# Router logits on four column groups, with start products and three smaller edits, in a two-model kernel on one Trainium2 core

## The chip, the cores and the metric

The kernel runs on one core of one Trainium2 chip. The metric is the device time of one execution in microseconds; lower is better. Everything is float32. TensorE handles a float32 product in several passes, which the trace keeps as two matmul records and two weight loads per product; a transpose has one of each.

## The reference, cut to what matters

Two models run one after the other on a sequence of 256 tokens of width 1024.

```python
def reference(...):
    x = first_block(x, ...)      # two hybrid layers: gated delta rule beside attention, LN, conv FFN, LN
    return second_block(x, ...)  # one layer: differential + dilated attention, then 16 experts

# inside second_block
x = x + jnp.concatenate([oa, od], axis=-1) @ w_out[l]
x = x + expert_choice_ffn(rms_norm(x, norm2_g[l]), w_router[l], w_gate[l], w_up[l], w_down[l])
return rms_norm(x, norm_f_g)

def expert_choice_ffn(h, w_router, w_gate, w_up, w_down):
    aff = jax.nn.softmax((h @ w_router).astype(jnp.float32), axis=-1)   # [1, 256, 16]
    g, idx = lax.top_k(aff.transpose(0, 2, 1), cap)                     # cap = 32 tokens per expert
    ...  # each expert: silu(xe @ wg) * (xe @ wu) @ wd, scaled by g, added at idx
```

The hidden width of an expert is 2816, so the weights of one expert are 34.6 MB and those of all 16 make up most of what the kernel reads.

## The kernel before, in words

Each engine has its own hand-written list of instructions; semaphores alone order them. Tokens are held as two tiles of 128 rows (`t` = 0, 1), channels as eight tiles of 128 (`k`). `x` holds rows, `xT` the transposed rows. PSUM is used as eight banks of 512 float32 columns, `ps[0]` to `ps[7]`.

**Start.** SyncE (queue SP) issues the first weights in an order written out: the first block of `first_in` (`first_columns`), half of `x_t` (`xT_in1`), the second block (`second_columns`), two more blocks (`slot_in0`), then the streams of `w_in` (line 375), unit 2 first, then unit 1 and unit 3. Only then come the convolution's coefficients `conv_w` (line 412, `conv_in`) and small vectors. TensorE starts in `first_products` (lines 823 to 838): it waits for the first columns, forms 16 products of 256 columns (line 826), 16 more (line 813), one for a table of biases (line 831), and 16 for unit 2 (line 676); then come the gate logits (line 901, 32-column weights), the first piece of dense work (line 861) and the key products (line 916). ScalarE waits for `conv_in` before its first tap (line 1482). VectorE first copies the bias table (line 1871), waits for `conv_in` too, and then runs the other taps (line 1881), on which the SiLU and the key products at line 916 depend.

**Around the router.** After the attention of the second model, TensorE forms the output product of tile 0 (into banks 2, 3), then that of tile 1 (banks 6, 7), line 1261, with the transposes of tile 0 (line 1236) inside. VectorE adds both halves of a tile to `x` (line 2208), ScalarE squares and copies the first transposed half (line 1648), VectorE the second (line 2211), and then applies the norm to 1024 columns (`rms`, line 2149) for the gather. `logits` (line 1244) holds 128 transposed tokens stationary and streams the 16 columns of `router_w`, eight products a tile. Then VectorE's `router_bias` (line 2219), ScalarE's Exp (line 1690), VectorE's `affinities` (line 2228), TensorE's two transposes (line 1270), VectorE's copies (line 2237) and the search of the 32 best of 256 (lines 2242 to 2248). TensorE fills waits with products whose result nobody reads (`keep_clock`, line 1251): one of 512 columns before the transposes, four behind them. The choice is transposed (line 1277), rows are gathered (line 1290), and expert 0 begins at line 1348.

**Experts.** 16 times: gate and up products (line 1348), 32 token columns stationary on each of four column groups, then the down products (line 1316), in two halves. Weights come in pieces of 5.6 MB into four slots; a DMA is issued when its slot's last reader (`piece_used`, for expert 0 also `first_columns_used`) is done. In the last expert the second half of the down weights comes in four transfers of 4, 4, 2 and 1 row blocks (`LAST_ROWS`, line 508), and TensorE waits for each.

The end: the placed rows (line 1404), the last norm (lines 1643 and 2154), the store.

Of the kernel before, what the change touches and what calls it, by code (L numbers as in the profile page):

```python
# [12 lines left out]
P = 128  # L13
S = 256
# [70 lines left out]

HID_BANKS, OUT_BANK = (3, 4, 6), (4, 0)


def constants():
# [35 lines left out]
    parts["slot"] = np.broadcast_to((np.arange(P) % CAP)[None, :] + 1, (P, P))  # L125
    at, cols = {}, 0
# [42 lines left out]
def build(nc, a, out, scratch, CAT):  # L169
    ctx = ExitStack()  # L170
    with ctx:
# [125 lines left out]
        normed_rows = second_scratch.take(T, D)  # L297
        out_quarters = second_scratch.take(D // 4)
        BIAS_BEFORE = 2 * H * 3 * P - T * D - D // 4
# [51 lines left out]
        def _(sp):  # L351
# [39 lines left out]
            for l in range(DEPTH):  # L391
# [12 lines left out]
                first_blocks(2, 4).then_inc(sem("slot_in0"), 16)  # L404
                for u in (2, 1) + tuple(range(3, len(UNITS_IN))):
                    name = UNITS_IN[u]
                    stream(l, u, columns(a["w_in"], l, OFF[name], AB_COLUMNS if name == "ab" else 512, u))
                    if u == RING - 1:

                        if l:  # L410
                            sp.wait_ge(sem("x_rows"), at(l, "x_rows", 2))
                        sp.dma_start(conv_w, a["conv_columns"][l]).then_inc(sem("conv_in"), 16)
# [231 lines left out]
        def _(pe):  # L644
# [586 lines left out]
            def rows_transposed(t):  # L1231

                pe.wait_ge(sem("second_rows"), t + 1)
                for kh in range(2):
# [4 lines left out]
            def logits(t, ks):  # L1239

                if ks[0] == 0:
                    pe.wait_ge(sem("h2_copied"), 2 * t + 2)
# [11 lines left out]
            for t in range(T):  # L1254
                for k in range(4):
                    if t == 0:
                        pe.wait_ge(sem("attended_read"), at(L, "attended_read", k + 1))
                    elif k == 1:
                        rows_transposed(0)
                    for nh in range(2):  # L1260
                        last = mm(ps[ROWS_BANKS[2 * t + nh]][:, :], mixT[:, 4 + k, t * P:(t + 1) * P], slot(7, 1024)[:, k, nh * 512:(nh + 1) * 512], start=(k == 0), stop=(k == 3))
                last.then_inc(sem("rows_used" if t else "rows_t0"), 2 if t else 1)
# [45 lines left out]
            def keep_clock_on_rows():  # L1308

                mm(ps[1][:, :], ident, normed_rows[:, 0, 0:512], start=True, stop=True)  # L1310
# [16 lines left out]
            def expert(n_, ahead):  # L1327
# [102 lines left out]
        def _(act):  # L1430
# [203 lines left out]
            def rms(n, t):  # L1634
# [3 lines left out]
                elif n == 1:  # L1638
                    act.wait_ge(sem("second_rows"), t + 1)
# [6 lines left out]
                if n == 1:  # L1646
                    act.wait_ge(sem("h2_transposed"), 2 * t + 1)
# [68 lines left out]
        def _(v):  # L1716
# [148 lines left out]

            for l in range(DEPTH):
# [332 lines left out]
            v.drain()  # L2199
            def second_rows(t):  # L2200
# [3 lines left out]
                else:  # L2204
                    v.wait_ge(sem("rows_used"), (DEPTH + 1) * ROW_UNITS + 2)
                for nh in range(2):
                    xs = x[:, t, nh * 512:(nh + 1) * 512]
                    last = w.tensor_add(xs, xs, ps[ROWS_BANKS[2 * t + nh]][:, :])
                last.then_inc(sem("second_rows"), 1)
                v.wait_ge(sem("h2_transposed"), 2 * t + 2)  # L2210
                w.tensor_copy(xT[:, 4:8, t * P:(t + 1) * P], ps[H2_BANKS[2 * t + 1]][:, :].rearrange("p (x y) -> p x y", y=P)).then_inc(sem("h2_copied"), 1)
                if t == 1:
                    router_bias(0)
                rms(1, t, normed_rows, "h2_rows")

            def router_bias(t):

                v.wait_ge(sem("logits"), t + 1)
# [130 lines left out]
```

## Time and profile before

| what | value |
|---|---|
| time, median of 3 runs | 2191.35 us (2190.85 to 2191.48) |
| time of the profiled execution | 2190.44 us |
| its span, first to last instruction | 2188.7 us |
| TensorE busy, share of the span | 1678.1 us, 77% |
| VectorE busy | 644.2 us, 29% |
| ScalarE busy | 310.7 us, 14% |
| read from memory | 692.77 MB |
| mean granted TensorE clock | 0.876 |

The span runs from the first to the last instruction; the execution's own time has 1.7 us around it. A share of busy time is a mean over stages with different limits: TensorE sets the pace up to about 945 us, the weights' transfers after it. In rows of the timeline the columns are start, duration, engine, line, operation, result and operand shape, count, and in brackets the idle time before with what ended it. In rows of windows "PEclk" is the clock granted to TensorE, 1.00 for 2.4 GHz and 0.50 for 1.2 GHz.

### The profile page before, as it was taken

To read this page: it belongs to the slowest core of one execution; us is meant where nothing else is said; L and a number is where in the kernel's file an instruction comes from. 1 tells how busy PE (TensorE), PEld (TensorE's weight loads), DVE (VectorE), ACT (ScalarE), POOL (GpSimd) and SP (SyncE) were. 2 spreads that over 40 slices of the span, in tenths; PEclk is the share of its full clock that TensorE was granted. 3 is DMA by queue.
4 is the path that set the end of the run, shared out by engine and by line. 5 is a ranking of instruction groups with operands and counts; after the bars stand their busy time and mean duration, and the time that the engine had idled before them with its cause. 6 is when DMAs were issued, how large, how long until landed. Compare 5 with 4: busy or idle time off the path is not lost.

```text
span 2188.7 us, 30640 instructions
## 1 busy us (share of the span) xinstructions
PE 1678.1 (77%) x13062; PEld 968.0 (44%) x13062; DVE 644.2 (29%) x1520; ACT 310.7 (14%) x739; POOL 255.5 (12%) x221
## 2 busy tenths in 40 slices
PE   8999999999999999995665565665656466466566
PEld 7867994886799476441221221221122122122122
DVE  3345777545477734320110010010010010010011
ACT  3231220324122013310000000000000000000001
POOL 0003880001388000000000000000000000000000
PEclk9999999999999999987777777777787777778778
DMA  8234652723554275489999999999999999999998
GB/s 316 79 116 145 215 181 96 255 79 116 164 173 175 96 263 235 200 374 430 433 433 434 431 427 434 435 435 434 433 426 433 435 435 434 434 431 427 435 434 345
DMA packets 99943, 695.12 MB, mean 318 GB/s; under 512 B 7627, under 2 KB 53067, under 8 KB 85773
## 3 DMA queue, kind: packets, MB, share of 16 engines
q1 hardware_dynamic: 96304, 684.71, 76.0%
q0 software_dynamic: 1712, 5.35, 0.7%
q10 hardware_dynamic: 1836, 3.80, 0.5%
q8 instruction: 64, 1.05, 0.2%
q14 instruction: 27, 0.21, 0.0%
HBM read 692.77 MB, written 4.22 MB: 318 GB/s over the span
## 4 chain that ended last, share of the span: by engine, by line
DMA 49%; PE 48%; DVE 1%; SPq 1%; ACT 1%; issue 0%; DVEq 0%; ACTq 0%
DMA arena<-in_gate_up 32%; DMA arena<-in_down_rows 17%; PE bank L1123 11%; PE bank L702 6%; PE bank L861 6%; PE bank L1348 6%; PE bank L676 3%; PE bank L1316 2%; PE bank L856 1%; PE bank L1182 1%; PE bank L1063 1%; PE bank L1186 1%; PE bank L1083 1%; PE bank L766 1%; PE bank L813 1%; PE bank L1209 1%
## 5 line engine op out<-in xcount | busy, mean ns | idle before, releaser
L1348 PE MATMUL bank<-arena 128*32 128x512 f32 (+1 forms) x3072 | 441.9, 741 | 366.0 <-DMA arena<-in_gate_up 365.5
L1348 PEld LDWEIGHTS bank<-arena 128*32 128x32 f32 x3072 | 112.5, 139 | 690.5 <-DMA arena<-in_gate_up 395.6
L2290 DVE TENSOR_TENSOR arena<-arena,bank 64x256 f32<-64x256 f32 x96 | 51.3, 535 | 766.3 <-ACT arena L1696 764.7
L1316 PE MATMUL bank<-arena 128*32 128x256 f32 x2816 | 204.5, 458 | 68.6 <-DMA arena<-in_down_rows 68.6
L1123 PE MATMUL bank<-arena 128*128 128x128 f32 x2128 | 238.0, 274 | 0.0
L1123 PEld LDWEIGHTS bank<-arena 128*128 128x128 f32 x2128 | 237.8, 192 | 0.0
L1316 PEld LDWEIGHTS bank<-arena 128*32 128x32 f32 x2816 | 101.0, 130 | 175.4 <-DMA arena<-in_down_rows 86.3
L861 PE MATMUL bank<-arena 128*128 128x256 f32 x576 | 138.6, 387 | 0.0
L1696 ACT ACTIVATE arena<-bank 64x512 f32<-64x512 f32 (+1 forms) x48 | 23.2, 550 | 809.0 <-PE bank L1348 809.0
L702 PE MATMUL bank<-arena 128*128 128x512 f32 x308 | 133.2, 592 | 0.0
L861 PEld LDWEIGHTS bank<-arena 128*128 128x128 f32 x576 | 104.7, 189 | 18.9 <-issue 4.6
L702 PEld LDWEIGHTS bank<-arena 128*128 128x128 f32 x308 | 57.8, 189 | 73.2 <-issue 70.1
L676 PE MATMUL bank<-arena 128*128 128x128 f32 (+1 forms) x704 | 87.0, 285 | 1.4 <-DVE arena L1770 1.4
L676 PEld LDWEIGHTS bank<-arena 128*128 128x128 f32 x704 | 84.1, 191 | 5.1 <-DVE arena L1770 2.6
L2126 DVE SCALAR_TENSOR_TENSOR arena<-bank,arena 128x254 f32<-128x254 f32 (+1 forms) x176 | 76.8, 478 | 24.8 <-ACT arena L1615 18.7
L1615 ACT ACTIVATE arena<-bank,arena 128x256 f32<-128x256 f32 x88 | 45.0, 562 | 139.0 <-DVE bank L2109 119.2
L536 POOL TENSOR_TENSOR arena<-arena 128x512 f32<-128x512 f32 x38 | 49.6, 1305 | 101.4 <-PE bank L1083 71.9
L1358 PE MATMUL bank<-arena 128*128 128x128 f32 x96 | 24.4, 342 | 48.3 <-DVE arena L2290 48.3
L539 POOL TENSOR_TENSOR arena<-arena 128x512 f32<-128x512 f32 x38 | 53.7, 1413 | 0.0
L2295 DVE COPY arena<-bank 64x256 f32<-64x256 f32 x16 | 6.9, 430 | 155.5 <-PE bank L1316 155.5
L538 POOL TENSOR_TENSOR arena<-arena 128x512 f32<-128x512 f32 x38 | 49.2, 1295 | 13.9 <-issue 8.6
L541 POOL TENSOR_TENSOR arena<-arena 128x512 f32<-128x512 f32 x38 | 49.6, 1306 | 5.4
(322 smaller groups left out, 1595.0 us busy)
## 6 DMA issues: line engine op xcount, KB each, us to landing
arena<-in_gate_up SPq DMA_DIRECT2D x60, 5632.0 KB, 46.2
arena<-in_down_rows SPq DMA_DIRECT2D x29, 5632.0 KB, 46.1
arena<-in_w_up SPq DMA_DIRECT2D x44, 1024.0 KB, 7.8
arena<-in_w_in SPq DMA_DIRECT2D x36, 1024.0 KB, 9.3
arena<-in_w_down SPq DMA_DIRECT2D x16, 1024.0 KB, 6.9
arena<-in_gate_up SPq DMA_DIRECT2D x5, 2816.0 KB, 12.3
arena<-in_w_out SPq DMA_DIRECT2D x12, 1024.0 KB, 6.1
arena<-in_w_down SPq DMA_DIRECT2D x12, 512.0 KB, 3.7
```

What stands on the lines that cost most here:

```text
L536: nc.gpsimd.tensor_tensor(s1, w[:, 0:4, cg], w[:, 4:8, cg], ALU.add)
L538: nc.gpsimd.tensor_tensor(s2, s1, w[:, 0:4, cv], ALU.subtract)
L539: nc.gpsimd.tensor_tensor(w[:, 0:4, cg], w[:, 0:4, cv], w[:, 0:4, cg], ALU.subtract)
L541: nc.gpsimd.tensor_tensor(s4, w[:, 4:8, cv], s2, ALU.subtract)
L676: last = mm(ps[bank][:, j * S + lo:j * S + lo + n], w[:, k, c:c + P], xT[:, k, lo:lo + n], start=(k == 0), stop=(k == KT - 1))
L702: return mm(ps[PRODUCT_BANK[m]][:, :], left, right, start=(i == 0), stop=(i == KP - 1))
L861: last = mm(ps[bank][:, j * S:(j + 1) * S], slot(u, 512)[:, k, c:c + P], xT[:, k, :], start=(k == 0), stop=(k == KT - 1))
L1123: last = mm(ps[pair[b]][:, at_ * P:(at_ + 1) * P], left[:, k, :], right[:, k, :], start=(k == 0), stop=(k == 3))
L1316: done = mm(ps[5][32 * q:32 * q + 32, 0:256], hidden_t[:, r, 32 * half:32 * half + 32], weights[:, r - shift, 256 * q:256 * q + 256], star ...
L1348: last = mm(ps[b][32 * q:32 * q + 32, 0:n], expert_x[:, k, :], weights[:, c:c + n], start=(k == 0), stop=(k == KT - 1))
L2126: last = w.scalar_tensor_tensor(ff_conv[:, j % 3, gv, s:S], from_, conv_w[:, 48 + c:49 + c], ff_conv[:, j % 3, gv, s:S], ALU.mult, ALU.add)
L2290: last = w.tensor_mul(hidden[64 * odd:64 * odd + 64, 2 * b:2 * b + m, :], blocks(expert_gate[0:64, c0:c0 + n]), blocks(ps[b][64:P, 0:n]))
```

## The change

Five edits are made together.

1. The logits. `router_w` (16 columns) becomes stationary on four column groups of the array, and 128 columns of `xT` stream past it. Channel tile `k` goes to group `k % 4`, so that four partial sums lie in partitions 0, 32, 64 and 96 of bank `2 + t`, columns 256 to 383. VectorE copies them out (`partials_copied`); one product with the copy stationary and a table of zeros and ones `by_group` adds the four and turns them. VectorE zeroes that part of the two banks once. The output product of tile 1 is ordered by halves of 512 columns, and each half is added and transposed by itself; VectorE takes ScalarE's copy for tile 1.
2. `keep_clock(1)` ahead of the affinities' transposes becomes `keep_clock(1, 2)`, 256 columns for 512.
3. Six products of zeros at the start (five of 256 columns, one of 128), after VectorE has set 256 columns of `zeros`.
4. For the first layer `conv_w` is loaded ahead of the `w_in` streams.
5. In the last expert three products of 512 columns, read by nobody, stand between the first and the second of the four groups of down products.

```diff
+START_PRODUCTS = (S, S, S, S, S, P)
+    parts["by_group"] = (i % 32 == np.arange(NE)[None, :]) * 1.0
...
                 first_blocks(2, 4).then_inc(sem("slot_in0"), 16)
+                if l == 0:
+                    sp.dma_start(conv_w, a["conv_columns"][l]).then_inc(sem("conv_in"), 16)
...
+                pe.wait_ge(sem("zeros_ready"), 1)
+                for n in START_PRODUCTS:
+                    mm(ps[7][:, 0:n], zeros[:, 0:P], zeros[:, 0:n], start=True, stop=True)
                 pe.wait_ge(sem("first_columns"), 16)
...
+            def rows_transposed(t, half=None):
+                for kh in range(2) if half is None else (half,):
+                    pe.wait_ge(sem("second_rows"), t + 1 + (kh if t else 0))
...
+            def partial_logits(t, ks):
+                pe.wait_ge(sem("h2_copied"), 2 if t == 0 else 4 if ks[0] == 0 else 5)
                 for k in ks:
-                    last = mm(ps[2 + t][:, 0:NE], xT[:, k, t * P:(t + 1) * P], router_w[:, k, :], start=(k == 0), stop=(k == KT - 1))
+                    g = 32 * (k % 4)
+                    last = mm(ps[2 + t][g:g + NE, S:S + P], router_w[:, k, :], xT[:, k, t * P:(t + 1) * P], start=(k < 4), stop=(k >= 4))
...
+            def logits(t):
+                pe.wait_ge(sem("h2_copied"), 3 * t + 3)
+                mm(ps[2 + t][:, 0:NE], logit_parts[:, t * P:(t + 1) * P], table("by_group"), start=True, stop=True).then_inc(sem("logits"), 1)
...
+            for nh in range(2):
                 for k in range(4):
+                    if nh == 0 and k == 2:
                         rows_transposed(0)
+                    if nh == 1 and k == 1:
+                        partial_logits(0, range(KT))
+                    last = second_product(1, k, nh)
+                if nh == 0:
+                    last.then_inc(sem("rows_t0"), 1)
+            last.then_inc(sem("rows_used"), 2)
+            rows_transposed(1, 0)
+            logits(0)
+            rows_transposed(1, 1)
+            partial_logits(1, range(4))
+            partial_logits(1, range(4, KT))
+            logits(1)
+            keep_clock(1, 2)
-            logits(0, range(6))
-            rows_transposed(1)
-            logits(0, range(6, KT))
-            logits(1, range(KT))
-            keep_clock(1)
...
                             last = down_rows(half, rows_, r0, n)
+                            if i == 0:
+                                for _ in range(3):
+                                    keep_clock_on_rows(4)
...
+            w.memset(zeros, 0.0).then_inc(sem("zeros_ready"), 1)
...
+            def partials_copied(t):
+                v.wait_ge(sem("logits"), 2 * t + 1)
+                w.tensor_copy(logit_parts[:, t * P:(t + 1) * P], ps[2 + t][:, S:S + P]).then_inc(sem("h2_copied"), 1)
...
+                    if t and nh == 0:
+                        partials_copied(0)
+                if t == 0:
+                    v.drain()
+                    w.memset(banks[:, 512 * 2:512 * 4].rearrange("p (b n) -> p b n", b=2)[:, :, S:S + P], 0.0)
+                    v.drain()
+                for kh in range(2):
+                    if t or kh:
+                        v.wait_ge(sem("h2_transposed"), 2 * t + kh + 1)
+                        w.tensor_copy(xT[:, 4 * kh:4 * kh + 4, t * P:(t + 1) * P], ps[H2_BANKS[2 * t + kh]][:, :].rearrange("p (x y) -> p x y", y=P)).then_inc(sem("h2_copied"), 1)
                 if t == 1:
+                    partials_copied(1)
                     router_bias(0)
                 rms(1, t, normed_rows, "h2_rows")
```

## Rows read from the trace of the kernel before

**Rows 1.** The chain that ended last, in order of time: start, duration, what.

```profile
15.64 11.49 DMA arena<-in_conv_columns
...
964.81 39.26 DMA arena<-in_gate_up
```

**Rows 2.** The timeline of the start, all engines, parts of the first 46 us.

```profile
1.27 0.42 SPq L400 DMA_DIRECT2D arena<-in_x_t  x1
...
5.79 9.74 PE L826 MATMUL bank<-arena 128*128 128x256 f32 x32 [5.79 <-DMA arena<-in_first_in]
...
15.37 7.09 PE L813 MATMUL bank<-arena 128*128 128x256 f32 x32
...
23.46 0.68 DVE L1871 COPY arena<-bank 12x512 f32<-12x512 f32 x1 [23.46 <-PE bank L831]
...
27.16 1.57 ACT L1482 ACTIVATE arena<-bank,arena 128x256 f32<-128x256 f32 x4 [10.26 <-DMA arena<-in_conv_columns]
...
28.11 8.10 DVE L1881 SCALAR_TENSOR_TENSOR arena<-bank,arena 128x255 f32<-128x255 f32 x18 [3.98 <-ACT arena L1482]
...
30.48 1.08 PE L901 MATMUL bank<-arena 128*32 128x256 f32 x16
...
34.26 1.15 PE L916 MATMUL bank<-arena 128*64 128x64 f32 x32 [0.22 <-ACT arena L1494]
```

**Rows 3.** Windows inside line 826: busy times with records, granted clock, DMA share, GB/s.

```profile
6.00:11.00 5.00, 5.00 (x12) 3.96 (x13) 0.00 (x0) 0.00 (x0) 0.00 (x0) 1.00 1.01 379
11.70:15.00 3.30, 3.30 (x17) 2.89 (x16) 0.00 (x0) 0.00 (x0) 0.00 (x0) 1.00 1.05 397
```

**Rows 4.** The DMA issue of the second half of x_t: size, us to landing.

```profile
arena<-in_x_t SPq DMA_DIRECT2D x1, 512.0 KB, 7.1
```

**Rows 5.** The timeline around the router, 928 to 942 us.

```profile
928.01 1.29 DVE L2208 TENSOR_TENSOR arena<-arena,bank 128x512 f32<-128x512 f32 x2 [1.51 <-PE bank L1261]
...
930.48 0.69 DVE L2211 COPY arena<-bank 128x512 f32<-128x512 f32 x1 [1.19 <-PE bank L1236]
...
931.65 1.29 DVE L2149 SCALAR_TENSOR_TENSOR arena<-arena 128x1024 f32<-128x1024 f32 x1
...
933.64 0.17 DVE L2219 TENSOR_REDUCE arena<-bank 128x1 f32<-128x16 f32 x1 [0.71 <-PE bank L1244]
...
934.82 0.23 DVE L2228 TENSOR_SCALAR arena<-arena 128x16 f32<-128x16 f32 x1
...
935.29 0.63 PE L1270 MATMUL bank<-arena 128*16 128x128 f32 x2
...
935.72 5.44 PE L1251 MATMUL bank<-arena 128*128 128x512 f32 x8
...
935.75 0.49 DVE L2237 COPY arena<-bank 16x128 f32<-16x128 f32 x2 [0.70 <-PE bank L1270]
...
941.09 0.29 PE L1277 MATMUL bank<-arena 16*128 16x16 f32 x2
```

**Rows 6.** Two windows of the same stretch; columns as in rows 3.

```profile
929.00:932.50 3.50, 2.94 (x26) 2.74 (x26) 2.15 (x6) 3.07 (x5) 0.00 (x0) 1.00 1.05 410
932.50:935.90 3.40, 3.40 (x12) 2.04 (x12) 1.62 (x8) 1.05 (x5) 0.00 (x0) 0.51 1.01 417
```

**Rows 7.** The timeline of the last expert's second half of down products.

```profile
2132.79 1.75 SPq L508 DMA_DIRECT2D arena<-in_down_rows  x4
...
2170.20 1.93 PE L1316 MATMUL bank<-arena 128*32 128x256 f32 x32 [0.44 <-DMA arena<-in_down_rows]
...
2175.10 4.86 PE L1316 MATMUL bank<-arena 128*32 128x256 f32 x56 [2.96 <-DMA arena<-in_down_rows]
```

**Rows 8.** The DMA issues behind it: size, us to landing.

```profile
arena<-in_down_rows SPq DMA_DIRECT2D x1, 1024.0 KB, 43.9
...
arena<-in_down_rows SPq DMA_DIRECT2D x1, 512.0 KB, 44.6
```

**Rows 9.** A window inside the last 56 records; columns as in rows 3.

```profile
2175.50:2178.00 2.50, 2.50 (x28) 1.18 (x24) 0.00 (x0) 0.00 (x0) 0.00 (x0) 0.50 0.36 147
```

More of the change, by code:

```diff
@@ L297, in build @@
         normed_rows = second_scratch.take(T, D)
+        zeros = normed_rows[:, 0, 0:S]
         out_quarters = second_scratch.take(D // 4)
+        logit_parts = out_quarters
         BIAS_BEFORE = 2 * H * 3 * P - T * D - D // 4
@@ L411, in _ @@
                             sp.wait_ge(sem("x_rows"), at(l, "x_rows", 2))
-                        sp.dma_start(conv_w, a["conv_columns"][l]).then_inc(sem("conv_in"), 16)
+                            sp.dma_start(conv_w, a["conv_columns"][l]).then_inc(sem("conv_in"), 16)
                         for i in range(2):
@@ L1253, in _, with second_product @@
             unit_in(L, 7)
-            for t in range(T):
+            def second_product(t, k, nh):
+                return mm(ps[ROWS_BANKS[2 * t + nh]][:, :], mixT[:, 4 + k, t * P:(t + 1) * P], slot(7, 1024)[:, k, nh * 512:(nh + 1) * 512], start=(k == 0), stop=(k == 3))
+            for k in range(4):
+                pe.wait_ge(sem("attended_read"), at(L, "attended_read", k + 1))
+                for nh in range(2):
+                    last = second_product(0, k, nh)
+            last.then_inc(sem("rows_t0"), 1)
+            for nh in range(2):
                 for k in range(4):
-                    if t == 0:
-                        pe.wait_ge(sem("attended_read"), at(L, "attended_read", k + 1))
-                    elif k == 1:
+                    if nh == 0 and k == 2:
                         rows_transposed(0)
-                    for nh in range(2):
-                        last = mm(ps[ROWS_BANKS[2 * t + nh]][:, :], mixT[:, 4 + k, t * P:(t + 1) * P], slot(7, 1024)[:, k, nh * 512:(nh + 1) * 512], start=(k == 0), stop=(k == 3))
-                last.then_inc(sem("rows_used" if t else "rows_t0"), 2 if t else 1)
-            logits(0, range(6))
-            rows_transposed(1)
-            logits(0, range(6, KT))
-            logits(1, range(KT))
-            keep_clock(1)
+                    if nh == 1 and k == 1:
+                        partial_logits(0, range(KT))
+                    last = second_product(1, k, nh)
+                if nh == 0:
+                    last.then_inc(sem("rows_t0"), 1)
+            last.then_inc(sem("rows_used"), 2)
[6 more added lines that the diff above has]
+            keep_clock(1, 2)
             for t in range(T):
@@ L1306, in _, with keep_clock_on_rows @@
             gathered_transposed(1)
-            def keep_clock_on_rows():
-                mm(ps[1][:, :], ident, normed_rows[:, 0, 0:512], start=True, stop=True)
+            def keep_clock_on_rows(bank=1):
+                mm(ps[bank][:, :], ident, normed_rows[:, 0, 0:512], start=True, stop=True)
             def down_rows(half, weights, r0, n, shift=0):
@@ L1645, in rms @@
                     f(normed_rows[:, t, :], x[:, t, :], ACT.Square, accum_out=sum_sq[:, t:t + 1])
-                if n == 1:
-                    act.wait_ge(sem("h2_transposed"), 2 * t + 1)
+                if n == 1 and t == 0:
+                    act.wait_ge(sem("h2_transposed"), 1)
                     f(xT[:, 0:4, t * P:(t + 1) * P], ps[H2_BANKS[2 * t]][:, :].rearrange("p (x y) -> p x y", y=P), ACT.Copy).then_inc(sem("h2_copied"), 1)
@@ L2203, in second_rows @@
                     v.wait_ge(sem("rows_t0"), at(L, "rows_t0", 1))
-                else:
-                    v.wait_ge(sem("rows_used"), (DEPTH + 1) * ROW_UNITS + 2)
                 for nh in range(2):
+                    if t:
+                        v.wait_ge(*((sem("rows_used"), (DEPTH + 1) * ROW_UNITS + 2) if nh else (sem("rows_t0"), at(L, "rows_t0", 2))))
                     xs = x[:, t, nh * 512:(nh + 1) * 512]
                     last = w.tensor_add(xs, xs, ps[ROWS_BANKS[2 * t + nh]][:, :])
-                last.then_inc(sem("second_rows"), 1)
-                v.wait_ge(sem("h2_transposed"), 2 * t + 2)
-                w.tensor_copy(xT[:, 4:8, t * P:(t + 1) * P], ps[H2_BANKS[2 * t + 1]][:, :].rearrange("p (x y) -> p x y", y=P)).then_inc(sem("h2_copied"), 1)
+                    if t or nh:
+                        last.then_inc(sem("second_rows"), 1)
+                    if t and nh == 0:
[8 more added lines that the diff above has]
+                        w.tensor_copy(xT[:, 4 * kh:4 * kh + 4, t * P:(t + 1) * P], ps[H2_BANKS[2 * t + kh]][:, :].rearrange("p (x y) -> p x y", y=P)).then_inc(sem("h2_copied"), 1)
                 if t == 1:
+                    partials_copied(1)
                     router_bias(0)
@@ L2216, in router_bias @@
             def router_bias(t):
-                v.wait_ge(sem("logits"), t + 1)
+                v.wait_ge(sem("logits"), 2 * t + 2)
                 w.tensor_reduce(rmax[:, t:t + 1], ps[2 + t][:, 0:NE], AX.X, ALU.max, negate=True)
```

8 lines of the change are left out of this document (1 added, 7 removed).

## The prediction

> **What bounds the kernel now.** I read the chain of waits first. In the first 16 us it ends in a transfer: the coefficients of the convolution, issued at 15.64 us, landing 11.49 us later. From about 31 to 945 us it is mostly TensorE's products, and from 964.81 us on it alternates between transfers of expert weights, the first of them 39.26 us, and the products that free their slots [rows 1]. So the kernel has two regimes. Up to 945 us whatever shortens TensorE's list moves all behind it. After that, weights flow without a gap; since each transfer is issued when a product has freed a slot, an earlier start of expert 0 moves the whole flow, and a gain inside the flow is worth nothing except behind the last transfer. The change works in three places: the start, the router (928 to 945 us), and the last 20 us. I read the timeline of each, then the landings of the transfers and the granted clock in windows.
>
> **The start: edits 3 and 4.** TensorE begins at 5.79 us. Its first 32 records take until line 813 begins at 15.37 us, 9.6 us, while the next 32 of the same shape take 7.02 us up to the bias product (15.37 + 7.09 less the overlap of the tail), which is 0.44 us a product [rows 2]. The windows say why: 12 records in 5.00 us, then 17 in 3.30 us [rows 3]. The column of the granted clock reads 1.00 in both, so here the counts must be believed and not the column: the first 5.8 us ran at 1.2 GHz. The Trainium skill's page "TensorE: Matmul & The Clock Gate", Part 1, says that the clock is low by default and that the engine's activity releases it; by that rule the operands' values would not matter, and the counts of rows 3 agree with the first half of it.
>
> The zero products need VectorE's memset; VectorE has nothing ahead of it (its first instruction in the trace waits for line 831 and starts at 23.46 us [rows 2]). I take 1.3 us for it to be done, the time at which SP issues [rows 2]. At the low clock a product of 256 columns takes 0.83 us (5.00 us / 12 records, two a product), so five and a half take 4.6 us and end at 5.9 us, where the first columns land: nothing is lost. If the clock is up by then, four products take 1.76 us and end at 7.7 us; the next four need the second half of `x_t`, issued at 1.27 us and landed 7.1 us later [rows 4], at 8.37 us. Twelve products follow: 8.37 + 12 x 0.44 = 13.65 us instead of 15.37, **a gain of 1.7 us**. Its bounds: 0.1 us lost (the fill runs from 5.79 to 5.9 and the clock stays low), and 2.1 us won (0.40 us a product, as 17 records in 3.30 us give).
>
> This gain alone would stop at line 916, the key products: they wait for ScalarE's SiLU with only 0.22 us of idle time for TensorE before them, and that SiLU hangs on the taps of VectorE, 28.11 to 36.21 us, which hang on the coefficients' landing at 27.1 us [rows 1, 2]. Edit 4 removes that. The transfer goes behind four of SP's issues instead of ten; I take the landing at about 13 us from its neighbours (8.37 us for an issue at 1.27). The first tap can then follow the first products at 13.65, and VectorE starts when the bias copy is done, about 22.5 us (23.46 - 1.7 + 0.7). Its 8.1 us of taps end some 4 us earlier than before, where TensorE comes only 1.7 us earlier: line 916 no longer waits. The issues that `conv_w` is moved past, the six of `w_in`, come one small transfer later, 112 KB, about 0.3 us at 397 GB/s [rows 3]; TensorE waits for none of them before 31 us, all its rows there being back to back. So edit 4 is worth 0.2 us by itself and opens the way for the 1.7 of edit 3; I count 1.7 together. Behind it TensorE's list is the chain.
>
> **The router: edits 1 and 2.** Product by product, against the times before. `partial_logits(0)` is put into tile 1's output product. The nearest row is line 901: eight products with 32 stationary columns and 256 moving ones between full products, 1.08 us [rows 2]. Half the columns take away up to 0.44 us: 0.6 to 1.1, I take 0.8. So the product ends at 928.8 instead of 928.0. The page "TensorEngine Tiling (Array Packing)" of the Trainium skill, Tiling Modes, Key Properties, says that a change of the tiling mode drains TensorE, which speaks against this edit; line 901 holds one such pair in its 1.08 us, tile 1's partial products would add a second of some 0.2 us (1.08 less 2 x 0.44), and by that rule edit 1 would gain nothing.
>
> Behind 928.8 only one addition of 0.65 is left (the other went ahead): 929.45, where two took until 929.30 [rows 5]. VectorE then copies both transposed halves, 0.69 each, one of which was ScalarE's: 930.85 against 931.17. The last four partial products and their hop 0.5 (bound 0.3 to 0.6, from half of line 901), their copy 0.28 as half of line 2237's pair: 931.65. From the end of the copy to the end of the norm's 1024 columns it took 1.77 us (931.17 to 932.94) and that stays, because VectorE's list is the same: 933.4, when the second `router_bias` can start. Before, it waited for TensorE's narrow logits until 933.64. So turning the logits gains **0.2 us**, not the 1.9 us by which TensorE's 16 records shrink: VectorE is at once the bound, with the norm of tile 1 in its queue.
>
> Then edit 2. The affinities are ready at 935.05, but the filler product held the transposes until 935.29 and the copies until 935.75 [rows 5]; half as long and started earlier, it is out of the way, and the copies come 0.45 us earlier beside the 0.2. The search of VectorE ends about 0.6 us earlier, at 940.3 or so. But the fill of four products, 935.72 + 5.44 = 941.16, ended with the search, at line 1277 (941.09). It took 5.44 us because the clock, full until 932.5, was 0.51 in the window behind it [rows 6]; at the full clock it would take 3.5. In the new order it starts 0.4 us earlier and ends, with the clock rising when it did, at 940.9. **Edits 1 and 2 together: 0.2 us.** Bounds: 0.8 won, where the search alone decides (clock full), and 1.1 lost, where all four products run at 1.2 GHz from 935.4 us: 4 x 1.7 us, to 942.2. The zeroing of banks 2 and 3 on VectorE costs nothing: it lies where VectorE waits for transposes of tile 0. Later `rows_used` makes SP issue two pieces 0.8 us later; expert 0 needs the first of them only two channel pairs into its products.
>
> **The end: edit 5.** Before the last seven row blocks TensorE was idle for 2.96 us; their 56 records took 4.86 us, to 2179.96, with the clock at 0.50 [rows 7, 9]. At the pace of the 32 before (1.93 us) they would take 3.4. Three products of 0.88 us fit into 2.96. But the transfers bound the gain: of four issues in 1.75 us the third starts at 2133.67 and lands 43.9 later, at 2177.6, the fourth at 2134.1 plus 44.6, at 2178.7 [rows 7, 8]. The first 32 records end at 2177.03, wait, the next 16 end at 2178.5, wait, the last 8 end at 2179.2. **Gain 0.8 us**, not 1.5. Bounds: 0.8, and 0 in an execution whose clock did not fall there.
>
> **The sum.** The profiled execution took 2190.44 us, 1.7 around its span. 2190.44 - 1.7 - 0.2 - 0.8 = 2187.7. The median of the runs lies 0.9 above that execution, so 2188.6 us.
>
> **Rivals.** (a) The router stage gives its bound: the clock does not fall and the search alone decides. 2188.6 - 0.6 = 2188.0. For it: the new order has fewer narrow products. Against it: the window in which the clock was lost had 2.94 us of 3.50 busy [rows 6], and the new order idles more there. (b) Products of zeros don't raise the clock, or not by 8.4 us: edit 3 gives nothing, edit 4 its 0.2: 2188.6 + 1.7 - 0.2 = 2190.1. No row shows a product of zeros. (c) The idle time ahead of the fill keeps the clock low through all four fill products, 1.1 lost instead of 0.2 won: 2189.9. For it: with the fill cut, TensorE stands still about 2 us there. (d) Slower: VectorE's memset comes late. TensorE waits for it before it may touch the first columns, so the start is z + 4.6 us for a memset at z, and line 813 begins at z + 11.6 (16 full-clock products). Against 15.37 this loses from z = 3.8 us, and the whole kernel from z = 4.8; at z = 9, for one, 2188.6 + 1.7 + 5.2 = 2195.5. Only that other engines issue by 1.3 us [rows 2] speaks against it.
>
> **Chances and range.** Forecast 0.58 (its own range 2187.6 to 2189.5); (a) 0.13; (b) 0.12; (c) 0.11; (d) 0.03; 0.03 for a cause that I don't see. All bounds won give 2190.44 - 2.1 - 0.8 - 0.8 + 0.9 = 2187.6; the runs spread by 0.6, and the 1233 us of weights' flow may differ by 0.04%, 0.5: down to 2186.5. Upward (b) and (c) with the same spread: 2190.8. About what a measurement of this kernel can tell from no change is 0.2%, 4.4 us. Nearly all cases lie within: faster by more 0.09 (all bounds and a cause unseen), same 0.87, slower 0.04.
>
> **What would show it.** Line 813 begins near 13.6, with line 826's records short from 8.4 on; line 1482 follows the first products, not a transfer; expert 0 (line 1348) begins near 943.6; line 2219's second record waits for nothing; line 1277 waits for the fill; in the last expert TensorE waits twice more, for the third and the fourth transfer, at a clock of 1.00. I am wrong if line 813 doesn't move, if line 1251's fill grows beyond 6 us, or if the shift of line 916 is lost before 945 us.

## The result and the profile after

The kernel after takes 2198.66 us (median of 7 runs, 2198.38 to 2199.62), the one before 2191.35 (7 runs, 2189.39 to 2194.5): a ratio of 1.0036, 95% interval 1.0026 to 1.0046. It is slower: 7.3 us between the medians, 0.33%. The forecast of 2188.6, its range up to 2190.8 and all four rivals miss it. The span of the profiled execution went from 2188.7 to 2196.8 us.

The first reading is where along the span the 8.1 us arise. Four marks do it: the start of the long dense part (line 1132; line 1123 before; called line 1132 for every kernel below), of tile 0's output product, of expert 0 (line 1373), and of the first of the last four groups of down products (line 1341; line 1316 before).

| stretch | before | after | change |
|---|---|---|---|
| start to line 1132 | 209.54 | 207.75 | -1.8 |
| line 1132 to the output product | 703.60 | 703.53 | -0.1 |
| output product to expert 0 | 32.36 | 31.47 | -0.9 |
| expert 0 to the first of the last four groups | 1224.7 | 1236.7 | +12.0 |
| from there to the end of the last group | 9.76 | 8.64 | -1.1 |

The three places that the change works on all gained. The loss is in the flow of the experts' weights, where the change does nothing until its last 20 us. The chain of waits shows how it is spread. After:

```profile
207.75 118.81 PE bank L1132 x1064
...
942.75 19.14 PE bank L1373 x192
962.05 39.34 DMA arena<-in_gate_up
...
1378.17 5.00 PE bank L1341 x88
...
1540.72 6.69 PE bank L1341 x88
...
1702.56 5.00 PE bank L1341 x88
...
1864.41 6.69 PE bank L1341 x88
```

Before:

```profile
1378.69 6.69 PE bank L1316 x88
...
1538.61 5.00 PE bank L1316 x88
...
1698.53 5.00 PE bank L1316 x88
...
1858.46 5.00 PE bank L1316 x88
```

One pass of the loop handles two experts. Before, it takes 159.92 or 159.93 us, three times over; after, 162.55, 161.84 and 161.85. So every pass pays about 2 us: it is no single stall. The queues of the DMA engines say what differs in a pass. Rows are queue and kind, packets, MB, share of 16 engines; first the window from 1445 to 1605 us of before, one pass long:

```profile
DMA packets 1730, 69.30 MB, mean 433 GB/s; under 512 B 192, under 2 KB 192, under 8 KB 192
...
q1 hardware_dynamic: 1730, 69.30, 100.3%
```

The same window of after:

```profile
DMA packets 1722, 68.95 MB, mean 431 GB/s; under 512 B 186, under 2 KB 186, under 8 KB 186
...
q1 hardware_dynamic: 1713, 68.80, 99.8%
q8 instruction: 9, 0.15, 0.4%
```

Queue q8 is named for instructions; its packets are of 16 KB (0.15 MB / 9). Before, it moved nothing in this pass, nor in any other from 1285 to 2085 us; after, it moves nine packets in each, in a stretch where the weights already take all 16 engines. Over the whole kernel q8 has 64 packets before and 118 after, on the pages of the two profiles. The row of before:

```profile
q8 instruction: 64, 1.05, 0.2%
```

And of after:

```profile
q8 instruction: 118, 1.93, 0.4%
```

The 54 more are six times nine. The loop runs seven times (the last two experts stand behind it), so after each of its six jumps back the body is fetched anew. 12.0 us over six is 2.0 us a pass, as the chain shows.

TensorE's list of instructions gives the cause that I put to the test. By count of the program, one pass of the expert loop is 1687 instructions of TensorE (a float32 product is four, a transpose two, two waits in a row one). The loop begins at instruction 13861 in before and at 13893 in after, 32 later: 24 for the six products of zeros, 8 for the logits' two added products. Nothing inside the loop is changed.

For the places of the change, the timeline of after; columns as in [rows 2]. The start:

```profile
0.88 0.27 DVE L1894 MEMSET arena<- 128x256 f32 x1 [0.88 <-PEq L2365]
1.21 4.49 PE L827 MATMUL bank<-arena 128*128 128x256 f32 x12 [1.21 <-DVE arena L1894]
...
2.94 0.48 SPq L410 DMA_DIRECT2D arena<-in_conv_columns  x1
...
5.79 2.00 PE L835 MATMUL bank<-arena 128*128 128x256 f32 x8
8.52 5.47 PE L835 MATMUL bank<-arena 128*128 128x256 f32 x24 [0.73 <-DMA arena<-in_x_t]
13.83 7.09 PE L819 MATMUL bank<-arena 128*128 128x256 f32 x32
...
22.52 5.41 DVE L1910 SCALAR_TENSOR_TENSOR arena<-bank,arena 128x255 f32<-128x255 f32 x12
...
32.36 1.13 PE L925 MATMUL bank<-arena 128*64 128x64 f32 x32
```

The memset is done at 1.15 us, the zeros' 12 records end at 5.70, as the first columns land, and the 32 records of line 835 (826 before) need 8.2 us with their wait instead of 9.74 [rows 2]. In the kernel without the products of zeros (run 3 below) the same 32 records take 9.26 us. The products of zeros do raise the clock. Around the router:

```profile
923.46 0.63 PE L1253 MATMUL bank<-arena 128*16 128x128 f32 x16
...
926.89 0.80 SPq L452 DMA_DIRECT2D arena<-in_gate_up  x2
...
931.53 0.17 DVE L2263 TENSOR_REDUCE arena<-bank 128x1 f32<-128x16 f32 x1
...
933.10 5.30 PE L1265 MATMUL bank<-arena 128*128 128x512 f32 x8
933.65 0.41 DVE L2286 MAX8 arena<-arena 16x8 f32<-16x256 f32 x1
...
938.33 0.30 PE L1302 MATMUL bank<-arena 16*128 16x16 f32 x2
```

The end, the answer to [rows 7]:

```profile
2179.46 1.93 PE L1341 MATMUL bank<-arena 128*32 128x256 f32 x32
2181.32 2.84 PE L1335 MATMUL bank<-arena 128*128 128x512 f32 x6
2184.09 1.93 PE L1341 MATMUL bank<-arena 128*32 128x256 f32 x32
2186.19 1.07 PE L1341 MATMUL bank<-arena 128*32 128x256 f32 x16 [0.16 <-DMA arena<-in_down_rows]
2187.46 0.64 PE L1341 MATMUL bank<-arena 128*32 128x256 f32 x8 [0.20 <-DMA arena<-in_down_rows]
```

A window inside it, the answer to [rows 9]: the clock is 1.00 where it was 0.50.

```profile
2184.00:2188.00 4.00, 3.64 (x57) 1.50 (x56) 0.00 (x0) 0.00 (x0) 0.00 (x0) 1.00 0.26 102
```

### The profile page after: what moved, and what is told of

The parts are those of the page before. It is cut to its first block, busy times and chain, and to the rows that moved or that the text cites. A ratio compares the mean times of both kernels' runs of the same rounds, so it can differ in the third digit from the quotient of the medians.

```text
span 2196.8 us, 30690 instructions
## 1 busy us (share of the span) xinstructions
PE 1682.7 (77%) x13084; PEld 968.7 (44%) x13084; DVE 645.6 (29%) x1525; ACT 310.6 (14%) x738; POOL 255.7 (12%) x221
## 4 chain that ended last, share of the span: by engine, by line
DMA 49%; PE 49%; DVE 1%; ACT 1%; issue 0%; DVEq 0%; SPq 0%; ACTq 0%
DMA arena<-in_gate_up 32%; DMA arena<-in_down_rows 17%; PE bank L1132 11%; PE bank L870 6%; PE bank L708 6%; PE bank L1373 6%; PE bank L682 3%; PE bank L1341 2%; PE bank L1191 1%; PE bank L865 1%; PE bank L1072 1%; PE bank L1195 1%; PE bank L1092 1%; PE bank L819 1%; PE bank L772 1%; PE bank L1218 1%
## 5 line engine op out<-in xcount | busy, mean ns | idle before, releaser
L542 POOL TENSOR_TENSOR arena<-arena 128x512 f32<-128x512 f32 x38 | 49.6, 1305 | 101.7 <-PE bank L1092 71.9
L545 POOL TENSOR_TENSOR arena<-arena 128x512 f32<-128x512 f32 x38 | 54.1, 1425 | 0.0
L544 POOL TENSOR_TENSOR arena<-arena 128x512 f32<-128x512 f32 x38 | 48.8, 1284 | 13.7 <-issue 8.4
```

What stands on the lines that cost most here:

```text
L542: nc.gpsimd.tensor_tensor(s1, w[:, 0:4, cg], w[:, 4:8, cg], ALU.add)
L544: nc.gpsimd.tensor_tensor(s2, s1, w[:, 0:4, cv], ALU.subtract)
L545: nc.gpsimd.tensor_tensor(w[:, 0:4, cg], w[:, 0:4, cv], w[:, 0:4, cg], ALU.subtract)
```

## The experiments

The theory, F: where the expert loop begins in TensorE's list decides whether its body is fetched again in every pass, and those fetches slow the flow of weights. Rival L: the added table `by_group` shifts the layout of memory or of the transfers. Further rivals put the loss on a part of the change itself, the products of zeros or the logits. Below, "flow" is the stretch from expert 0 to the first of the last four groups (1224.7 us before), and "shift" is how many instructions later than before the loop begins.

**1. The shift alone.** The kernel before, with 64 waits that are already satisfied (32 instructions) put ahead of TensorE's first wait. Nothing is computed differently.

```diff
+                for _ in range(64):
+                    pe.wait_ge(sem("rows_used"), 1)
                 pe.wait_ge(sem("first_columns"), 16)
```

> The kernel before with 32 waits on a semaphore that is already high at the head of TensorE's list, where it stands idle for 5.8 us; nothing else. Its expert loop so begins 32 instructions further on, as in the changed kernel. Theory F (the loop of 1687 instructions, shifted, covers one more 16 KB block of instructions and is fetched again in every pass): the queue that fetches instructions carries about 9 packets in each 160 us of the expert stage instead of 0, the stage loses about 11 us, the time is near 2202. Theory L (the constants' table, 16 columns wider, shifts every tile and array, and the transfers of weights run slower for that): no packets, 2191 as before.

Measured: 2203.26 us (4 runs, 2201.72 to 2205.09) against 2190.53, ratio 1.0054 (1.0038 to 1.0071). The flow takes 1235.25 us. The queues in the window from 1445 to 1605 us:

```profile
q1 hardware_dynamic: 1719, 68.80, 99.8%
q8 instruction: 9, 0.15, 0.4%
```

That the list grew by 32 instructions is seen on the pages, which count 30640 for before and 30672 for this kernel. The nine packets and 10.5 us of the loss in the flow are there without any part of the change. The start is slower too: TensorE's first product begins at 6.32 us instead of 5.79, and line 1132's part begins 3.1 us later; why the 0.5 grow to 3.1 was not followed up. So this kernel is slower than after by more than the gains that it lacks; the flow is the figure to compare.

**2. The table alone.** The kernel before, with `by_group` added to its constants and read by nobody.

```diff
+    parts["by_group"] = (i % 32 == np.arange(NE)[None, :]) * 1.0
```

> The kernel before with the table by_group of 16 columns added to the constants, unread; all tiles shift as in the changed kernel, no engine's list changes. Theory F: no packets in the expert loop, 2191. Theory L: about 11 us slower, 2202.

Measured: 2192.02 us (10 runs, 2190.58 to 2193.93), ratio 1.0007 (0.9997 to 1.0016); flow 1225.65, q8 64 packets. Rival L falls.

**3. The change without the products of zeros.** The shift is then 8 instructions, those of the logits.

```diff
-                pe.wait_ge(sem("zeros_ready"), 1)
-                for n in START_PRODUCTS:
-                    mm(ps[7][:, 0:n], zeros[:, 0:P], zeros[:, 0:n], start=True, stop=True)
```

> The changed kernel without the six start products and their wait, so that the expert loop begins 8 instructions behind its place in the kernel before instead of 32; the start products' 1.8 us are given up. Theory F: if the border lies more than 8 instructions behind the old place (3 in 4 when it is anywhere in the 32), no packets in the loop, and 2198.7 + 1.8 - 11 = 2189.5. If the border is nearer, 9 packets per 160 us and 2200.5. Theory L: 2200.5 without packets.

Measured: 2191.03 us (10 runs, 2189.26 to 2194.95), ratio 1.0003 (0.9994 to 1.0013); flow 1226.5, no q8 packet in a pass. It was expected at 2189.5. By itself this could also mean that the products of zeros do harm. Its start gives a number for edit 4 alone: line 1132's part begins at 208.85, 0.7 earlier than before.

**4. All of the change, and 168 more instructions.** If F holds, *more* instructions at the right number make the kernel faster. Waits already satisfied are strewn among the down products of the second layer.

```diff
+                    if l == 1:
+                        for _ in range(6 if i < 2 else 4):
+                            pe.wait_ge(sem("rows_used"), 1)
                     return mm(ps[PRODUCT_BANK[m]][:, :], left, right, start=(i == 0), stop=(i == KP - 1))
```

> The changed kernel with 168 waits that are already met, strewn into the down products of the second layer, two or three ahead of a product of 0.43 us, so that the loop begins 168 instructions further on, in the next block. All work is the same, only the list is longer. Theory F: no packets in the loop, 2198.7 - 11 = 2188 if the waits hide behind the products. Theory L: not faster than 2198.7.

Measured: 2188.04 us (10 runs, 2187.5 to 2189.97) against 2190.53, ratio 0.9989 (0.998 to 0.9999). Flow 1226.1. The page of its profile:

```profile
q8 instruction: 64, 1.05, 0.2%
```

This is the strongest run of the study: every instruction of the change is still there, the products of zeros too, and 10.6 us are back. It also clears the fifth edit and the logits of harm in the flow, and it is the fastest version found.

**5. The parts, with the loop in a good place.** Two kernels with the loop exactly where run 4 has it (shift 200): run 4 without edit 5, and the kernel before with edits 3, 4 and 5 but the old logits and `keep_clock(1)`.

```diff
-                            if i == 0:
-                                for _ in range(3):
-                                    keep_clock_on_rows(4)
```

The other one, before with edits 3 to 5 (the rest of its edits is as in the change), keeps these lines:

```diff
             logits(0, range(6))
             rows_transposed(1)
             logits(0, range(6, KT))
             logits(1, range(KT))
             keep_clock(1)
```

> e4_after_long without edit 5, the three products ahead of the second transfer of the last expert; the expert loop stays where it is in e4. The transfers bound the end: the records behind the wait run at 1.2 GHz again, the stretch from the first of the four groups to its end grows from 8.9 us to 9.8, and the time by 0.8 to 1.1 us on 2188.0. If the edit's products were worth nothing, the time stays at 2188.0.

> e4_after_long with edits 1 and 2 undone (the logits, the order of the output product and the filler as in the kernel before), edits 3 to 5 kept, and 176 waits for 168, so that the loop begins at the same instruction as in e4. By my forecast the router's edits are worth 0.2 us: 2188.2. By the traces (31.4 us from tile 0's output product to expert 0 in e4, 32.4 to 33.3 in the kernels with the old order) they are worth 1.0 to 1.9: 2189.0 to 2189.9.

Without edit 5: 2189.29 us (11 runs, 2187.82 to 2190.17), 1.25 above run 4, though the two sets of runs overlap; the spans of the profiled executions differ by 0.9 (2187.2 and 2186.3). Its timeline shows the old wait of [rows 7] come back:

```profile
2168.72 1.93 PE L1344 MATMUL bank<-arena 128*32 128x256 f32 x32
...
2173.64 4.92 PE L1344 MATMUL bank<-arena 128*32 128x256 f32 x56 [2.99 <-DMA arena<-in_down_rows]
```

With the old logits: 2188.51 us (11 runs, 2187.03 to 2191.61), 0.5 above run 4; from tile 0's output product to expert 0 it takes 32.37 us, as before (32.36), where run 4 takes 31.41. Edits 1 and 2 are worth 1.0 us in this pair of profiles and 0.5 by medians whose runs overlap, below the 1.0 to 1.9 that was expected from the traces. The profiles of all kernels together say it more firmly: counted from the first product's row of the timeline (913.07 us before), the stretch takes 32.4 to 33.4 us in the seven with the old order and 31.4 to 32.0 in the seven with the new.

**6. Other shifts.** The kernel before with more satisfied waits in the same products: 140, 264 and 288 instructions. Under F the length of the list as such doesn't matter, only where the loop lies within blocks of 256 instructions, so 264 should act as 8, and 288 as 32. One run each; N stands for the number.

```diff
+                    padded[0] += 1
+                    for _ in range(2 * (N // 154 + (padded[0] <= N % 154))):
+                        pe.wait_ge(sem("rows_used"), 1)
```

> The kernel before with 140 waits that are already met, spread over the down products. Theory F with a loop of 1687 instructions, which fits seven blocks of 256 from 106 of the 256 places and needs eight from the other 150: still inside the bad stretch (it began between 8 and 32 and ends between 158 and 182), so 9 packets in 160 us and about 2202. If the bad places were a few around 32 only: none, 2191.

> The kernel before with 264 waits that are already met, spread over the down products of both layers: the loop begins 264 = 256 + 8 instructions later. Theory F, in which the place modulo a block of 256 decides: as for a shift of 8, no packets in the loop, about 2191. If it were the length of the list and not the place: packets, about 2201, since 32 more sufficed.

> The same with 288 = 256 + 32 waits. Theory F: 9 packets in 160 us, about 2201, as for a shift of 32. If a longer list as such is safe (e4 was): no packets, about 2191.

Measured: 2201.64, 2193.84 and 2204.94 us, with before at 2191.15, 2190.42 and 2190.42. The queue on the pages of g264 and, behind it, of g288:

```profile
q8 instruction: 74, 1.21, 0.2%
```

```profile
q8 instruction: 119, 1.95, 0.4%
```

288 is 118 packets and one for a longer list: refetched in every pass, flow 1237.2. 264 is 64, one for the longer list, and nine of one single pass, between 1125 and 1285 us; its flow is 1228.2 and its time 2193.84 where 2191 was expected, so "as 8" holds but for that one pass. 140 has the nine in a pass and a flow of 1235.5.

**7. The products of zeros in fewer instructions.** Three of 512, 512 and 384 columns in place of six, the same columns in sum: 12 instructions fewer, shift 20.

```diff
-START_PRODUCTS = (S, S, S, S, S, P)
+START_PRODUCTS = (512, 512, 384)
-        zeros = normed_rows[:, 0, 0:S]
+        zeros = normed_rows[:, 0, 0:512]
```

> The changed kernel with the same 1408 columns of start products in three products (512, 512, 384) for six, on 512 columns of zeros: 12 instructions fewer, so that the loop begins 20 instructions behind its old place. Theory F knows the border only as between 8 and 32. If it lies above 20: no packets in the loop and 2188.0, as e4, with no wait added. If below: 9 packets in 160 us and 2198.7.

Measured: 2191.41 us (11 runs), ratio 1.0007 (0.9998 to 1.0016). The profiled execution, the fastest of the 11, has no packet in a pass, flow 1226.5 and a span of 2186.8, 1.9 below before. But the runs spread from 2188.71 to 2199.03, where run 4's spread by 2.5, and the median misses the 2188.0 expected without packets. A remedy that should have kept the whole gain keeps it only in some executions.

All shifts together:

| shift | kernel | q8 packets in a pass | flow us | time us |
|---|---|---|---|---|
| 0 | before | 0 | 1224.7 | 2191.35 |
| 0 | with the table | 0 | 1225.65 | 2192.02 |
| 8 | no products of zeros | 0 | 1226.5 | 2191.03, up to 2194.95 |
| 20 | three products of zeros | 0 | 1226.5 | 2191.41, up to 2199.03 |
| 32 | after | 9 | 1236.7 | 2198.66 |
| 32 | before and 32 | 9 | 1235.25 | 2203.26 |
| 140 | before and 140 | 9 | 1235.5 | 2201.64 (1 run) |
| 200 | run 4, the two of run 5 | 0 | 1225.4 to 1226.1 | 2188.04 to 2189.29 |
| 264 | before and 264 | 9 in one pass | 1228.2 | 2193.84 (1 run) |
| 288 | before and 288 | 9 | 1237.2 | 2204.94 (1 run) |

Packets and flow go together through the whole table, and neither follows the length of the list: 200 is good, 140 is bad.

**8. Why do 0.4% of the engines cost 1.2% of a pass?** To see what small transfers cost the flow, run 4 gets 26 copies of 16 KB per pass on ScalarE's queue, memory to memory, in one form as one row, in the other as 16 rows of 1 KB. What is copied is read by nobody; the copies' operands are shortened here to names.

```diff
+            def small_copies():
+                for i in range(13):
+                    act.dma_start(copy_to, down_rows_16_kb).then_inc(sem("small_copied"), 16)
...
             with act.Fori(0, NE - 1) as e:
                 expert(e)
+                act.wait_ge(sem("small_copied"), e * 208 + 208)
+                small_copies()
```

> e4_after_long (no fetches in the loop) with 26 copies of 16 KB in each pass, issued by ScalarE, memory to memory, each one row of 16 KB; the copies are read by nobody. In the changed kernel 9 packets of 16 KB cost 2.0 us a pass, while their bytes at 432 GB/s would cost 0.34. Theory S (a packet holds one of the 16 DMA engines for 1.1 us, and the bulk transfers wait for the slowest engine): the flow grows by some 4 us a pass or more, 30 us in all. Theory B (bytes alone): 26 x 16 KB, read and written, 2 us a pass, 14 us in all.

> The same 26 copies of 16 KB in each pass, each as 16 rows of 1 KB, which fall on many engines. Theory S: the cost of h1 falls to what the bytes ask, 14 us in all or less. Theory B: as h1.

Measured: 2197.15 and 2197.88 us (one run each), with flows of 1234.7 and 1235.9, 8.6 and 9.8 above run 4. The window from 1445 to 1605 us has this row in both:

```profile
q10 hardware_dynamic: 832, 0.43, 0.9%
```

Both forms were cut into 832 packets of 512 bytes, so the pair can't tell what it was made for, one 16 KB packet on one engine against the same bytes spread. What it does show: a load of 0.9% of a pass of 160 us, 1.4 us of all 16 engines, costs 8.6 to 9.8 us over the eight pairs of experts, 1.1 to 1.2 us each. Such transfers cost about the engine time that they take, less than either theory expected (14 and 30 us in all). The fetches take 0.4%, 0.64 us, and cost 2.0.

The traces show where most of the difference lies. Each transfer of weights ends in 16 packets below 512 bytes, 192 in a pass of 12 transfers, as the rows above count them. In before the 16 of one transfer start within 3.2 us, here from 1934.6 to 1938.0 us:

```profile
DMA packets 48, 1.44 MB, mean 424 GB/s; under 512 B 16, under 2 KB 16, under 8 KB 16
```

After has eight of them between 1932.5 and 1933.4 us, none from 1933.4 to 1941.9, and the other eight between 1941.9 and 1944.3:

```profile
DMA packets 17, 0.41 MB, mean 451 GB/s; under 512 B 8, under 2 KB 8, under 8 KB 8
```

```profile
DMA packets 83, 3.71 MB, mean 437 GB/s; under 512 B 0, under 2 KB 0, under 8 KB 0
```

```profile
DMA packets 30, 0.99 MB, mean 413 GB/s; under 512 B 8, under 2 KB 8, under 8 KB 8
```

The distance from the first to the last of the 16 stays at 3.2 us in before, at 3.45 in run 4 and at 3.1 to 3.3 with the small copies. It grows from 3.1 us (at 1132 us) to 13.2 (at 2013) in after, about 1.8 us a pass, and likewise in run 1 and at a shift of 140; at 264, with one refetched pass, it grows once, to 6.4, and stays. In after the early eight keep the period of run 4, 160.0 us a pass, and the late eight don't. TensorE waits for the last of the 16: its row at 1378.17 us in the chain of after follows a last packet at 1377.6, where the first had come at 1372.4. So with the fetches, 1.08 us each, half of every transfer falls behind and sets the pace, while the small copies leave the 16 together.

## Why the prediction was wrong

**The step that failed** is the assumption of a stable flow: "an earlier start of expert 0 moves the whole flow", and in the range "the 1233 us of weights' flow may differ by 0.04%, 0.5". The flow differs by 12.0 us, 1%. Behind it lies a cost counted as nothing without being named: the instructions that the change adds ahead of the loop. I priced each by its time on the engine and looked at nothing else that it does; 32 of them move the loop to where its body is fetched again in six passes. Even without fetches 0.5 us was too narrow: the flow takes 1224.7 to 1226.5 us in the profiles with none in a pass. Run 1 (those 32 alone give the loss) and run 4 (168 more take it away) show it from both sides. No rival of the prediction had this mechanism. The profile before held one clue, read by me too late: q8 with 64 packets in all, none of them from 1285 to 2085 us, where TensorE runs the loop again and again, so its body stayed in the engine's own memory, and whether it fits was a question to ask.

The Trainium skill, page "Runtime: NRT & Kernel Launch", section "Instruction fetch mechanics", says that TensorE holds 2048 instructions, filled in blocks of 256. By that the picture is: the 1687 instructions of a pass touch seven or eight blocks, by where they begin, and somewhere between the two the body no longer stays. The runs agree with the block of 256 (8 and, but for one pass, 264 against 32 and 288) and with packets of 16 KB. They leave two things open: 2048 instructions are eight blocks, which a body of eight should still fit, and a pass fetches nine. The page adds that the cost of crossing a block is "mostly hidden"; here the measurement decides, and it is about 2.0 us in each pass of 160, in a stretch where the weights take all the engines that the fetches use.

**Edits 3 and 4, the start: right.** Forecast 1.7 us, with line 813 (819 after) at 13.65. Line 819 begins at 13.83, 1.5 earlier, and line 1132 1.8 earlier. The wait for the second half of `x_t` came as written (8.52 forecast as 8.37). Line 925 begins at 32.36, 1.9 earlier than line 916 did [rows 2], and the coefficients are no longer waited for. One step there was reckoned wrong without harm: 22.5 + 8.1 puts the end of VectorE's taps at 30.6, not "some 4 us earlier" than 36.21; they ended at 32.67. The shares were off: edit 4 alone gave 0.7, not 0.2, and edit 3 the other 1.1. Of the 0.7, 0.5 arise in line 826's own records (9.26 us for 9.74), which edit 4 doesn't touch; with one profile of each, that part may be chance.

**Edits 1 and 2, the router: right in mechanism, too small in size.** Against before's times less the 1.86 us by which this stage begins earlier: `rows_used`, by SP's issue at 926.89, is where 928.8 put it. The eight partial products took 0.63 us, by their row and at the lower bound of my 0.6 to 1.1, with both changes of the tiling mode inside. The second `router_bias` is 0.25 earlier (0.2 forecast) and waits for nothing. The search begins 0.8 earlier (0.65 forecast). Mis-sized is the fill: it begins 0.76 earlier, not 0.4, and took 5.30 us, where the forecast's start and end leave 5.6; the choice is transposed 0.9 us earlier where I forecast 0.2. As the prediction says, it waits for the fill, which ends at 938.40. The 0.9 us of the stage is the size that rival (a) gave, but not by its mechanism: the clock reads 0.66 from 933 to 938 us and the fill, not the search, decides. Rival (c) falls too.

**Edit 5, the end: right.** Forecast 0.8 us, measured 0.9 to 1.3 from the profiles with it (before 9.76, then 8.64, 8.89, 8.97 and, without the products of zeros, 8.47), and 1.25 between the medians of runs 4 and 5. TensorE waits for the third and the fourth transfer, 0.16 and 0.20 us, at a clock of 1.00. It is more than my 0.8 because the last two transfers landed sooner: the products behind them begin 6.7 and 8.0 us behind the start of the first group, where I had 7.4 and 8.5. The lower bound of the prediction, no gain where the clock did not fall, shows as well: in the kernel before with 264 more waits the same stretch takes 8.58 us without edit 5, at a clock of 1.00.

**Rivals (b) and (d): both refuted.** The products of zeros raise the clock, and the memset is done at 1.15 us, far from the 3.8 at which it starts to lose.

**The sum.** With the measured terms, 2188.7 - 1.8 - 0.9 - 1.1 + 12.0 = 2196.9 for the span; it is 2196.8. Without the refetch, run 4's span is 2186.3, 0.3 above what my sum gives for a span (2188.7 - 1.7 - 0.2 - 0.8 = 2186.0), and its median of 2188.04 lies 0.6 below the forecast. That closeness is partly luck. In run 4 the three places gain 1.9, 1.0 and 0.9, 3.8 us in all where I had 2.7, and its flow, without a fetch, is 1.4 longer than before's. The local accounting had the right mechanisms and was too small at the router; the placement of the loop, worth 10.6 to 12, was not in it.

**What stays open.** Why the nine fetches cost three times their share of the engines (2.0 against 0.64 us a pass) is shown in part: half of each transfer falls behind. The profile doesn't name a packet's engine, so that the late half is on the engines that fetch is inferred; nine packets of 1.08 us on eight engines would be 1.2 us each, less than the 1.8 by which they fall behind. Exactly where the borders lie was not searched: one is between 20 and 32 and another between 140 and 200. That the wide spread of the runs at 20, the slow ones at 8 (2193.84 and 2194.95), the single refetched pass at 264 and the two odd runs of before (2193.94 and 2194.5) have one cause, a loop near a border that is refetched now and then, fits them all but is argued, not shown: no slow execution of these was profiled. The shift of after was not repaired inside the change, for example by a shorter list; run 7 tried, and its place is still one where single runs are slow.

## What to carry to other kernels

A loop that is nearly as long as an engine's instruction memory has a price for its *place*: instructions added anywhere ahead of it, or taken away, can change the time of a part that nobody touched. Before adding even cheap instructions, count the loop's length and where it begins, and look at the rows of the instruction queue inside one pass; if it is empty, keep it empty, and afterwards check it first. When a change gives its small gains where they were forecast and the total still goes the other way, compare the period of an untouched loop before looking at the edits: a shift by instructions that do nothing separates place from content in one run.

## What the runs showed of the hardware

- Instructions are fetched by a DMA queue that shares the engines with the data: with nine packets of 16 KB in a window of 160 us the weights' bytes in it fell from 69.30 to 68.80 MB, and the pass grew from 159.92 to about 161.9 us.
- A bulk transfer lands with its latest part: in after eight of a transfer's 16 closing packets came up to 13.2 us behind the first, about 1.8 us more in each pass, where before has 3.2 throughout. Copies of 0.9% of the engines' time that were spread evenly left it at 3.2 and cost 1.1 to 1.2 us a pair of experts.
- Satisfied waits cost TensorE nothing that can be measured between products of the dense part (168 instructions in the second layer, run 4: expert 0, behind them, begins at 942.55 us, in after at 942.75; it already was 0.14 ahead at 207.61 us), but with 32 at the head of the list the first product came 0.53 us later.
- The products of zeros raised the clock: line 835's first eight records took 2.00 us, 0.50 us for two, where 12 records of before took 5.00 us [rows 3]. The granted clock reads 1.00 in both stretches, so in the first microseconds the counts tell more than that column.
- A memory-to-memory copy of one row of 16 KB was cut into 32 packets of 512 bytes (832 packets for 26 copies), and so were 16 rows of 1 KB.
